# A convolution stage on Trainium2: four gate slots, weight loads ahead of their waits, weights rounded on ScalarE

## The reference, cut to what matters

```
h = rmsnorm(x) ; proj = h @ w_in          # 1024 -> 11264 columns
u = a_val * sigmoid(a_glu)
u = causal depthwise conv of u, width 31, + bias
u = silu(layernorm(u)) * silu(a_gate) ; y_a = u @ w_conv_proj
o = retention of q, k, v, normed, gated   # 2048 columns
y_b = o @ w_ret_proj                      # done in two halves of 1024 rows
m = sigmoid(g_a) * y_a + sigmoid(g_b) * y_b
x = x + m @ w_out
```

## Time and profile before

| | us |
|---|---|
| median of 3 runs (5366.49 to 5373.93) | 5370.01 |
| profiled execution, its own time | 5357.28 |
| its span | 5355.5 |
| PE busy in it | 4788.8 (89%) |
| DVE busy | 2458.1 (46%) |
| ACT busy | 1146.4 (21%) |
| POOL busy | 1300.3 (24%) |
| mean clock granted to TensorE | 0.929 |

### The profile page before, as it was taken

One profiled execution on the slowest core, in us unless ns is written; L12 is line 12 of the kernel. 1 busy time (PEld: TensorE's weight loads), 2 busy tenths in 40 slices (PEclk: granted clock), 3 DMA queues, 4 the chain that ended last, 5 costly groups with the idle time before them and its releaser, 6 DMA issues. The chain is left out here.

```text
span 5355.5 us, 56997 instructions
## 1 busy us (share of the span) xinstructions
PE 4788.8 (89%) x22876; PEld 3730.6 (70%) x22876; DVE 2458.1 (46%) x2420; ACT 1146.4 (21%) x1387; POOL 1300.3 (24%) x644
## 2 busy tenths in 40 slices
PE   5999888889999999984898999999999899997877
PEld 4888776768777786863576786877777566665556
DVE  6454555351212212999455424324242344447762
ACT  3323222011111111110201212112121222225410
POOL 1222113132213131561232322222131111112121
PEclk7999997889999999996998999899998999998988
DMA  3111213121111111220331101011010211116441
GB/s 101 56 55 55 74 63 115 47 80 43 63 42 64 46 59 56 63 94 32 122 118 70 60 13 56 26 39 40 32 50 16 75 59 61 62 33 226 151 165 48
DMA packets 115602, 365.22 MB, mean 68 GB/s; under 512 B 12917, under 2 KB 14469, under 8 KB 115273
## 3 DMA queue, kind: packets, MB, share of 16 engines
q1 hardware_dynamic: 83104, 297.15, 16.6%
q10 hardware_dynamic: 32296, 65.11, 3.2%
HBM read 267.62 MB, written 94.58 MB: 68 GB/s over the span
## 5 line engine op out<-in xcount | busy, mean ns | idle before, releaser
L442 POOL CAST b_w_hi<-b_w 128x1024 fp32r<-128x1024 f32 x277 | 343.4, 1240 | 3649.1 <-PE ps L509 2931.1
L509 PE MATMUL ps<-b_hi,b_w_hi 128*128 128x512 f32 x1920 | 780.9, 407 | 162.8 <-POOL b_w_lo L444 102.1
L509 PE MATMUL ps<-b_lo,b_w_hi 128*128 128x512 f32 x1920 | 757.7, 395 | 0.0
L509 PE MATMUL ps<-b_hi,b_w_lo 128*128 128x512 f32 x1920 | 757.6, 395 | 0.0
L444 POOL TENSOR_TENSOR b_w_lo<-b_w,b_w_hi 128x1024 fp32r<-128x1024 f32 x277 | 734.3, 2651 | 22.1
L509 PEld LDWEIGHTS ps<-b_hi,b_w_hi 128*128 128x128 f32 x1920 | 366.5, 191 | 263.7 <-issue 118.7
L509 PE MATMUL ps<-h_hT_hi,b_w_hi 128*128 128x512 f32 x1216 | 518.7, 427 | 17.7 <-PEq L95 4.5
L509 PE MATMUL ps<-h_hT_lo,b_w_hi 128*128 128x512 f32 x1216 | 488.3, 402 | 0.0
L509 PE MATMUL ps<-h_hT_hi,b_w_lo 128*128 128x512 f32 x1216 | 487.6, 401 | 0.0
L509 PEld LDWEIGHTS ps<-b_lo,b_w_hi 128*128 128x128 f32 x1920 | 367.4, 191 | 82.7 <-issue 9.3
L509 PEld LDWEIGHTS ps<-b_hi,b_w_lo 128*128 128x128 f32 x1920 | 366.7, 191 | 78.1
(11 more groups left out here) (632 smaller groups left out, 7521.5 us busy)
## 6 DMA issues: line engine op xcount, KB each, us to landing
b_w<-in_w SPq DMA_DIRECT2D x277, 512.0 KB, 3.7
scratch_x_park<-xT SPq DMA_DIRECT2D x24, 512.0 KB, 4.1
xT<-scratch_x_park SPq DMA_DIRECT2D x16, 512.0 KB, 6.7
scratch_gate_park<-ret_fill_out ACTq DMA_DIRECT2D x32, 256.0 KB, 2.0
scratch_o_park<-ret_o ACTq DMA_DIRECT2D x16, 512.0 KB, 4.0
scratch_gate_park<-rw_fill_out ACTq DMA_DIRECT2D x32, 256.0 KB, 2.2
scratch_sb_park<-rw_fill_out ACTq DMA_DIRECT2D x32, 256.0 KB, 2.0
scratch_xz_park<-sb_fill_out ACTq DMA_DIRECT2D x32, 256.0 KB, 2.1
```

Source lines behind the costliest of these rows:

```text
L442: pool.tensor_copy(hi, w).then_inc(self.rounded, 1)
L509: ins = pe.matmul(out[:, t], w, y, start=start, stop=stop)
```

## The change

`norm_and_first_tile` cuts tile 1 too, on POOL, after its share of the halves. In retention and RWKV the cut at the start goes away; in retention each cut moves up by one place, so that the second tile of the convolution stage is cut at the end of the retention stage. In `conv_and_projection` the cast of a weight tile moves from POOL to ACT (`round_tile`), POOL keeps the subtraction (`subtract_tile`), the gate buffer gets four slots, and SP's queue is reordered.

```diff
             for k in range(1, KD, 2):
                 cut_h(pool, k)
+            stream.cut_tile(pool, 1)
...
+    def round_tile(self, act, k):
+
+        s = k % self.RING
+        act.wait_ge(self.done, 4 * (k + 1 - self.RING))
+        act.wait_ge(self.loaded[s], 16 * (k // self.RING + 1))
+        act.activation(self.w_hi[:, s, :], self.w[:, s, :], ACT.Copy).then_inc(self.rounded, 1)
+
+    def subtract_tile(self, pool, k):
+
+        s = k % self.RING
+        pool.wait_ge(self.rounded, k + 1)
+        pool.tensor_tensor(self.w_lo[:, s, :], self.w[:, s, :], self.w_hi[:, s, :], ALU.subtract).then_inc(self.cut, 1)
...
-            stream.cut_units(pool, 0, tiles, units)
+            stream.cut_units(pool, 1, tiles, units)
...
-        if e >= 2:
-            sp.wait_ge(added, e - 1)
-        sp.dma_start(sg[:, e % 2, :], gates[(first + e) * P:(first + e + 1) * P, :]).then_inc(g_loaded[e % 2], 16)
+        if e >= ring:
+            sp.wait_ge(added, e + 1 - ring)
+        sp.dma_start(sg[:, e % ring, :], gates[(first + e) * P:(first + e + 1) * P, :]).then_inc(g_loaded[e % ring], 16)
...
-            for e in range(2):
+            for e in range(4):
                 load_gate(sp, e, added)
             for e in range(KD):
                 stream.load(sp, base + stream.RING + e)
-                if e + 2 < KD:
-                    load_gate(sp, e + 2, added)
+                if 3 <= e < KD - 1:
+                    load_gate(sp, e + 1, added)
...
                 for t in range(nt):
-                    stream.cut_tile(pool, first_tile + 1 + nt * u + t)
+                    if nt * u + t:
+                        stream.subtract_tile(pool, first_tile + 1 + nt * u + t)
...
-                    stream.cut_tile(pool, base + 1)
+                    stream.subtract_tile(pool, base + 1)
...
             for e in range(1, KD):
-                stream.cut_tile(pool, base + 1 + e)
+                stream.subtract_tile(pool, base + 1 + e)
...
                     act.activation(dst[:, :], bank(n), fn).then_inc(evacuated, 1)
+                    stream.round_tile(act, first_tile + n + 2)
...
                 act.activation(stream.y_hi[:, k, :], mixed[:, k, :], ACT.Copy).then_inc(y_rounded, 1)
+            for e in range(1, KD):
+                stream.round_tile(act, base + 1 + e)
...
             early = nt + FIRST // 16 + 2
-            stream.cut_tile(pool, RW_UNIT)
```

More of the change, by code:

```diff
@@ L1937, in gated_products @@
 def gated_products(core, stream, base, sg, g_loaded, gates, first):
+    ring = len(g_loaded)
     def load(sp, e, added):
-        if e >= 2:
-            sp.wait_ge(added, e - 1)
-        sp.dma_start(sg[:, e % 2, :], gates[(first + e) * P:(first + e + 1) * P, :]).then_inc(g_loaded[e % 2], 16)
+        if e >= ring:
+            sp.wait_ge(added, e + 1 - ring)
+        sp.dma_start(sg[:, e % ring, :], gates[(first + e) * P:(first + e + 1) * P, :]).then_inc(g_loaded[e % ring], 16)
     def add(dve, e, out, dst, accumulate, gated, added):
-        s = e % 2
-        dve.wait_ge(g_loaded[s], 16 * (e // 2) + 16)
+        s = e % ring
+        dve.wait_ge(g_loaded[s], 16 * (e // ring) + 16)
         dve.wait_ge(stream.done, 4 * (base + e + 1))
@@ L2039, in conv_and_projection @@
         sig, val, gate, odd = (st.sb(n, [P, T]) for n in ("sig", "val", "gate", "odd"))
-        sg = st.sb("sg", [P, 2, T])
-        g_loaded = [st.sem("g_loaded0"), st.sem("g_loaded1")]
+        sg = st.sb("sg", [P, 4, T])
+        g_loaded = [st.sem(f"g_loaded{s}") for s in range(4)]
         o_loaded = [st.sem(f"o_loaded{k}") for k in range(KD)]
```

## The result

The changed kernel takes **5330.36 us** (median of four runs, 5319.59 to 5341.58), beside 5368.25 us for the kernel before in the same session: ratio 0.9928, 95% interval 0.9909 to 0.9947. That is 38 us faster, where the prediction had 59.9 off 5370.0. The time lies 4.4 us above the upper end of the range (5326). A later set of five runs gave a median of 5319.87 us (5291.38 to 5330.40; ratio 0.9901, 0.9886 to 0.9916). In the first set its runs spread over 22 us and in the second over 39, where the kernel before spread over 8 and 16. The profiled execution of the first set, read here, took 5341.58 us with a span of 5339.6: it is the slowest of the nine.

A forecast was written before the change was run, and what follows sets the result against it. DVE was taken to bound the convolution units, and late projection loads behind a waiting gate load the tail. Gains of 46.5 (convolution stage) and 13.4 (retention and RWKV starts), 59.9 off 5370.0, gave 5310.1 us; range 5299 to 5326.

The forecast's parts named there:

- Start of the convolution stage: Convolution stage's second tile, cut already in retention: PE no longer waits for POOL, DVE starts 7.9 us earlier.
- Gates: SP's queue: projection weight loads no longer wait behind gate loads; PE has four tiles left after T, not five.
- Casts on ACT: Convolution units 0 to 6: 23 casts no longer lengthen DVE's taps, -18.2 us; three more subtractions there, +6.4.
- T: Moment DVE takes projection products 0 and 1: forecast 2488.1, or 2481 less retention's 6.9; before 2507.98.
- The tail: Projection after T: PE has four tiles left, tile 7's cut is held, DVE takes product 7 by 2547.9.
- the forecast's last wait: Last sixteen taps: PE waits about 9 us for tile 7's cut, its POOL subtraction taking over 10 us.
- rival 2: Projection's tail: tile 6's subtraction is held as well as tile 7's; stage end near 2558.8, 5321 us; 0.17 with its like.
- rival 1: Projection's tail: POOL gets in during the last taps, tile 7 cut at about 2519; 5303.4 us; chance 0.22.
- Rival 3: Units 1 to 6: lone POOL subtractions not let in between taps; +128 us less some 50, 5448; chance 0.03.
- rival 4: SP's queue: the gates do nothing, another wait keeps loads back; only casts and starts count, 5330.5 us; chance 0.04.
- Starts of retention and RWKV: First tiles of both stages: PE's wait for tile 1's cut goes; gain 6.9 and 6.5, together 13.4 us.
- The sum: Whole kernel: 46.5 us from the convolution stage plus 13.4 from the starts, 59.9 in all: 5310.1 us; chance 0.52.

The follow-up runs named there:

- run 5: Changed kernel plus one more wait in every fourth convolution tap, so DVE's queue runs dry for a moment: 5311.65 us, ratio to before 0.9887.
- run 6: Changed kernel with the roundings left on POOL, plus a wait (gap) in every fourth convolution tap: 5334.79 us, ratio to before 0.9931.
- run 3: Kernel before with only the convolution stage's weight casts moved from POOL to ACT, two gate slots and starts as before: 5389.87 us, ratio 1.0044.
- run 8: The changed kernel measured again, unaltered, in a later set of five runs: 5319.87 us, ratio to before 0.9901.
- run 1: Kernel before with only the second weight tile cut in the norm stages and ahead of the convolution stage: 5354.30 us, ratio 0.9976.

## Why the prediction was wrong

**Start of the convolution stage: right.** 17.79 us of idle time for 18, PE's first wait for POOL gone.

**Gates: right.** Loads ahead of the waits; alone -25.2 us of stage. It did the most.

**Casts on ACT: right in its numbers, wrong in a premise.** No tap of 2.06 us is left, and runs 5 and 6 measure 19.7 us for the 18.2. But the whole sum stood on the sentence that "all the other POOL instructions of the stage got in after the tap in progress", and that is the step that failed. I had one refusal before me, the 16.07 us cast, and laid it to its place: sixteen taps behind L1953 with no TENSOR_SCALAR between. The trace had more in it, 13.4 us of DVE without a lengthened tap ahead of this cast, but I compared places in the code and not how long DVE had been running. In its place the runs showed instructions held for up to 31.1 us (32 of 66 that arrived more than 6.5 us into a run of DVE), and 19.7 us saved for the roundings only where gaps let POOL in.

T itself hides this. It was forecast at 2481 and came at 2491.35, but 8.5 of these 10 us were there at the pads' clearing. Counted from there T came at 369.4 us for 367.7, and that is luck: DVE was through with unit 6 already at 337.0, having run clean, as a held POOL lets it, and then waited 32.4 us for PE. What was lost was PE's lead. At T it had just ended tile 0, not tile 3.

**The tail: wrong for what it started with.** It took 82.4 us from the first product to the end against the forecast 59.8, and these 22.6 are nearly all of the 24.3 by which the stage missed. The forecast left four tiles to PE after T; there were seven, 76 us at 10.9. Tiles 4 and 6 were held, not tile 7, but this cost PE only 1.96 us, so neither the forecast's last wait nor rival 2 is what happened. With gaps the tail took 54.0 (run 5), near rival 1's 53.1.

**Rival 3 was the right one to fear, at the wrong price.** "A lone POOL subtraction is not let in between taps": it had 0.03 and 128 us. Its evidence against, the subtraction at 2381.90, was weak: it arrived four taps behind a lengthened one, so it would always have got in. The price was too high because I let PE stop in each unit and DVE wait for it every time; in the trace four units of seven were hit, PE had units of lead to lose before DVE felt it, and DVE gained 2.1 us for each subtraction that wasn't in its way. Rounding alone costs 21.5 us of stage (run 3). In hindsight, with this case at 24 us the range would have had to reach to 5334 and would have held the result. That the measured 5330.4 is so near rival 4's 5330.5 is chance: rival 4 has the gates do nothing, and they did the most.

**Starts of retention and RWKV: shown at the first tile, not settled as a whole.** In the changed kernel's trace the idle time before the second tile is gone and retention's tile 1 is evacuated 6.7 us earlier against the stage's start, as forecast (6.9). But at the end of retention nothing of it was left: the pads are cleared at 2121.92, before at 2120.36. Over all profiles, the pads are cleared at 2120.2 on average in the ten kernels with the starts and at 2123.4 in the four without (3.2 earlier); from the last product to the end it is 2759.1 against 2768.9 (9.8 less). Together 13.0, for 13.4, but the closeness is luck: single profiles lie up to 8 us off the first average, and up to 23 off the second, and without run 8's profile alone the sum is 9.6.

**The sum.** The forecast's stage of 427.5 us is what run 5 measured (427.6), but two differences cancel in it: T came 6.0 us later after the pads' clearing, about what the gaps cost, and the tail was 5.8 us shorter, since no tile was held. Its 5310.1 us lie between the two medians of that kernel, 5311.65 and 5308.91. The change as written misses the stage by 24.3 us in one profile and 13.8 in the other, and run 5 shows that this goes with the held subtractions. In the first profile the rest of the miss is 8.5 us ahead of the stage and 11.3 behind it. TensorE was at 1.2 GHz for 24 us longer than in before's profile in each of the two parts (283 against 259 us, and 391 against 367, summed over the trace's clock records), which at half speed is up to 12 us each. So the clock can account for the rest; what moved it isn't shown.

## What to carry to other kernels

Where a long back-to-back stream on VectorE with two SBUF inputs runs beside GpSimd, look at how long the stream has run when each GpSimd instruction arrives, not only at what an instruction of it costs. Here a pause that cost 0.11 us every eight to fourteen instructions was worth 14 to 26 us by the medians (18 to 29 of stage), since a held instruction mostly stayed out until the stream paused by itself. And taking work off the engine that was the nuisance can make what is left of it wait: by the table, each of its instructions had also shortened the run that the next one met.

A part is best timed in the stage that it changes. The stage's length told parts of 4 us apart, where the whole times of one kernel in one set lay 6 to 39 us apart (run 1's lone one aside). That holds for kernels in which little is held; the changed kernel's own stage moved by 10.5.

## What the hardware showed that I had not expected

**GpSimd kept out for 31 us.** The Trainium skill, page "SBUF — State Buffer", section "Who interferes with whom", says that whoever issues first has the shared pair for the whole instruction and that the other fully blocks. By that a subtraction waits for one tap; the 307 that came within 6.5 us of a pause or a lengthened tap do agree (up to 1.15 us of waiting). The 32 held ones don't: up to 24 DVE instructions passed a waiting POOL instruction. The measurement decides: of those that came after 8.5 us of unbroken run all 17 were passed by later DVE instructions, and of those between 6.5 and 8.5 us 15 of 49. What in the chip counts this run, and whether it is time or instructions (six clean taps are 7.2 us), wasn't told apart by any run; all taps here are of one size.

**TensorE's clock makes more of the scatter than the stage.** The two profiles of the changed kernel differ by 50.2 us of span. Of these 9.6 are there at the pads' clearing, 10.5 in the stage, and 30.1 behind it. Behind it TensorE was at 1.2 GHz for 391 us in the first and 319 in the second, which at half speed is up to 36 us. The stretches 2920 to 3300 and 3300 to 3700 of the first (upper pair) and the second profile (lower pair), the clock is the third number from the end:

```profile
2920.00:3300.00 380.00, 357.56 (x1923) 287.84 (x1923) 135.58 (x140) 81.21 (x94) 106.54 (x51) 0.94 0.12 41
3300.00:3700.00 400.00, 372.80 (x2101) 305.95 (x2099) 146.06 (x164) 82.59 (x103) 106.83 (x50) 0.93 0.11 39
```

```profile
2920.00:3300.00 380.00, 357.59 (x1947) 287.53 (x1947) 147.84 (x152) 81.31 (x95) 105.14 (x50) 0.97 0.13 43
3300.00:3700.00 400.00, 373.32 (x2245) 310.12 (x2244) 134.42 (x162) 80.39 (x103) 102.95 (x49) 0.96 0.11 36
```

PE is as busy, 357.6 and 373 us, but granted 0.97 and 0.96 of its clock instead of 0.94 and 0.93, and does more matmuls in the same time. PE's waits there are nearly the same (the longest groups, on DVE, 13.3 and 10.6 us, are equal); which of them is followed by a spell at 1.2 GHz is not. I have no run that says what sets that.
